# The roots of a norm spread by four transposes instead of a product with ones, and thirteen transposes of the identity at the start of TensorE's program

## The reference

```
n    = rmsnorm(x, ln1_g)                 # x * rsqrt(mean(x*x) + eps) * g
proj = n @ w_in                          # 1024 x 1536: pool, RG-LRU, gate
y_pool = pool_mixer(proj[:, :512])
y_lru  = rg_lru(conv(proj[:, 512:1024])) * gelu(proj[:, 1024:])
h    = x + concat(rmsnorm(y_pool), rmsnorm(y_lru)) @ w_out
h    = h + (silu(n2 @ w_gate) * (n2 @ w_up)) @ w_down      # n2 = rmsnorm(h)
out  = rmsnorm(h, lnf_g)
```

## Time and profile before

| what | value |
|---|---|
| runs of the kernel | 892.46, 892.58, 893.38 us (median 892.58) |
| profiled execution | 893.27 us |
| its span, first to last instruction | 891.4 us |
| PE busy | 880.2 us |
| DVE, ACT, POOL busy | 619.0, 394.1, 266.7 us |

### The profile page before, as it was taken

The page is one execution under the profiler, slowest core; times in us unless marked ns, Lnnn a source line. Parts: engine busy times, 40 slices in busy tenths (PEclk is TensorE's granted clock), DMA queues, the critical chain, the costliest instruction groups (busy, mean ns, idle before and its releaser), DMA issues.

```text
span 891.4 us, 11039 instructions
## 1 busy us (share of the span) xinstructions
PE 880.2 (99%) x3968; PEld 724.3 (81%) x3968; DVE 619.0 (69%) x866; ACT 394.1 (44%) x650; POOL 266.7 (30%) x208
## 2 busy tenths in 40 slices
PE   7999999999999999999999999999999999999997
PEld 6877788888888888888888888888888888888886
DVE  4778996655997956656565564655738975787667
ACT  6689733524555333233233232233334444454456
POOL 0000032723334555545555545555540000000000
PEclk9999999999999999999999999999999999999999
DMA  9033011133002423224232232423339933333334
GB/s 316 16 95 95 24 48 48 47 118 95 1 1 60 142 82 120 94 83 161 65 130 83 95 130 86 140 71 106 112 100 384 393 98 94 95 97 102 98 83 189
DMA packets 94318, 98.01 MB, mean 110 GB/s; under 512 B 5764, under 2 KB 63672, under 8 KB 94264
## 3 DMA queue, kind: packets, MB, share of 16 engines
q1 hardware_dynamic: 83736, 78.16, 26.2%
q10 hardware_dynamic: 10528, 19.15, 7.2%
HBM read 70.81 MB, written 24.38 MB: 107 GB/s over the span
## 4 chain that ended last, share of the span: by engine, by line
PE 98%; DMA 0%; DVE 0%; ACT 0%; issue 0%; DVEq 0%; ACTq 0%
PE bank L2212 23%; PE bank L2210 23%; PE bank L2211 23%; PE bank L2089 5%; PE bank L2096 5%; PE bank L2093 5%; PE bank L2018 3%; PE bank L2020 3%; PE bank L2019 3%; PE bank L2119 1%; PE bank L2061 1%; PE bank L2031 1%; DMA h<-in_x 0%; PE bank L2040 0%; PE bank L2102 0%
## 5 line engine op out<-in xcount | busy, mean ns | idle before, releaser
L751 POOL TENSOR_TENSOR r_lo<-gu_raw,r_hi 128x512 fp32r<-128x512 f32 x84 | 114.8, 1367 | 86.1 <-ACT r_hi L1051 86.1
L2210 PE MATMUL bank<-T_hi,r_lo 128*128 128x512 f32 x352 | 136.9, 389 | 0.0
L2211 PE MATMUL bank<-T_lo,r_hi 128*128 128x512 f32 x352 | 136.9, 389 | 0.0
L2212 PE MATMUL bank<-T_hi,r_hi 128*128 128x512 f32 x352 | 136.9, 389 | 0.0
L751 POOL TENSOR_TENSOR r_lo<-wsum_S,r_hi 128x512 fp32r<-128x512 f32 x66 | 98.1, 1487 | 114.8 <-ACT r_hi L1051 108.1
L2211 PE MATMUL bank<-d_lo,h_hi 128*128 128x512 f32 (+1 forms) x312 | 120.5, 386 | 0.0
L2212 PE MATMUL bank<-d_hi,h_hi 128*128 128x512 f32 (+1 forms) x312 | 120.5, 386 | 0.0
L2210 PE MATMUL bank<-d_hi,h_lo 128*128 128x512 f32 (+1 forms) x312 | 120.5, 386 | 0.0
L1051 ACT CAST r_hi<-gu_raw 128x512 fp32r<-128x512 f32 x84 | 52.0, 622 | 148.7 <-PE bank L2212 143.8
L2210 PE MATMUL bank<-nT_hi,r_lo 128*128 128x512 f32 x248 | 96.5, 389 | 0.0
L2211 PE MATMUL bank<-nT_lo,r_hi 128*128 128x512 f32 x248 | 96.5, 389 | 0.0
(11 more groups left out here) (250 smaller groups left out, 1610.2 us busy)
## 6 DMA issues: line engine op xcount, KB each, us to landing
h_raw<-hid_ops ACTq DMA_DIRECT2D x72, 256.0 KB, 2.6
gu_raw<-in_w_ffn_gate SPq DMA_DIRECT2D x22, 512.0 KB, 3.8
gu_raw<-in_w_ffn_up SPq DMA_DIRECT2D x22, 512.0 KB, 4.8
hid_ops<-hid SPq DMA_DIRECT2D x44, 256.0 KB, 2.3
dn<-in_w_ffn_down SPq DMA_DIRECT2D x44, 256.0 KB, 9.7
hid_ops<-hsum_S SPq DMA_DIRECT2D x33, 256.0 KB, 2.6
w_raw<-in_w_in SPq DMA_DIRECT2D x11, 512.0 KB, 4.4
h<-in_x SPq DMA_DIRECT2D x8, 512.0 KB, 6.5
```

The source lines that it names most:

```text
L751: pool.tensor_tensor(lo_of(n)[:], a_block(f, name), f32(hi_of(n)[:]), ALU.subtract)\
L2210: pe.matmul(bank, s_lo, m_hi, start=(opens and j == 0), stop=False, skip_group_check=True)
L2211: pe.matmul(bank, s_hi, m_lo, start=False, stop=False, skip_group_check=True)
L2212: ins = pe.matmul(bank, s_hi, m_hi, start=False, stop=(closes and j == n - 1), skip_group_check=True)
```

## The change

Two things, in one diff. (1) `diag` becomes `wide`: DVE multiplies ones instead of the identity by the root, so that each block has the root of a token in all columns of its partition, and TensorE transposes the four blocks into the four quarters of the bank. (2) TensorE no longer waits for the gains first: when `ident` is there it transposes `ident` seven times into bank 3, turns the gains, and transposes `ident` six more times. Bank 3 is not read before a later product opens it afresh.

```
-        diag = at("diag", 152.25, [P, HALF])
+        wide = at("wide", 152.25, [P, HALF])
...
             for t in range(4):
-                dve.tensor_scalar(diag[:, cols(t)], ident[:], rstd[:, t:t + 1], None, ALU.mult).then_inc(diag_ok, 1)
+                dve.tensor_scalar(wide[:, cols(t)], ones_sq[:], rstd[:, t:t + 1], None, ALU.mult).then_inc(wide_ok, 1)
...
+            def spin(times):
+                for _ in range(times):
+                    pe.transpose(psum[3][:, 0:P], ident[:], ident[:])
+
             pe.wait_ge(consts, 1)
+            spin(7)
             pe.wait_ge(g_rows_in, 16)
             pe.transpose(psum[2][:, 0:KT], g_rows[:], ident[0:KT, 0:KT]).then_inc(gT_ok, 1)
+            spin(6)
             for t in range(4):
                 first_transposes(t)
             project(0, 0)
...
             def broadcast_roots():
-                pe.wait_ge(diag_ok, 4)
-                pe.matmul(pg[0][:], ones_sq[:], diag[:], start=True, stop=True).then_inc(bcast_ok, 1)
+                pe.wait_ge(wide_ok, 4)
+                for t in range(4):
+                    ins = pe.transpose(pg[0][:, cols(t)], wide[:, cols(t)], ident[:])
+                ins.then_inc(bcast_ok, 1)
```

More of the change, by code:

```diff
@@ L288, in hymba_pool_rglru_block @@
         abs_ok, decay_ok = sem("abs_ok"), sem("decay_ok")
-        diag_ok = sem("diag_ok")
+        wide_ok = sem("wide_ok")
         var_ok = sem("var_ok")
```

## The result

The changed kernel takes 894.4 us (median of 22 runs, 892.28 to 896.55), the kernel before 893.05 us in the same comparison (22 runs, 892.42 to 893.7). The ratio is 1.0015, with a 95% interval of 1.0009 to 1.0021: slower, by a little, where 891.9 us and a range up to 893.0 had been predicted. The profiled execution of after took 893.95 us, with a span of 892.1 us, against 893.27 and 891.4 us before: this pair of traces differs by 0.7 us, the medians by 1.35, so the traces show where time goes and not the whole of the difference of the medians.

A forecast was written before the change was run, and what follows sets the result against it. PE, busy 880.2 of 891.4 us, was taken as the bound, with the start held by the low clock and loads of x. 893.27 - 0.96 (start) - 0.42 (roots) = 891.89, predicted 891.9 us, range 891.2 to 893.0.

The forecast's parts named there:

- 9.1 computed: Start: tile 3 of x lands at 9.10 us and becomes what bounds PE's transposes.
- part 1: Start: the thirteen identity transposes bring TensorE's clock rise forward, gaining 0.96 us that lasts to the end.
- rival 3: After the start: gaps let the clock fall back, products take 0.46 instead of 0.23 us; 6 us low gives 894.9; chance 0.04.
- Start: 0.96: Start: ACT's first `nT_hi` begins at 9.30 in place of 10.26 us, 0.96 us earlier, passing through to the end.
- 7.5: Start: TensorE's clock rises near 7.5 us; any rise up to about 8.1 us gives the same result.
- 0.15: Start: ACT begins about 0.15 us behind the start of the last transpose it needs.
- the gain was to be 0.3: Start, against the median of before: of a 0.7 us gain, 0.4 is the roots and the rest the start.
- lucky executions: Start: where the clock rises early, the old kernel too is held by tile 3, not under 892.31 us.
- Roots: 0.42: Roots: four transposes in place of the product with ones (0.86 us) save PE 0.42 us.
- Rival 1: Start: identity transposes don't bring the clock's rise forward; 892.98 us in an execution like the profiled one; chance 0.10.
- Less spread between executions: Whole kernel: run times should vary less than before, whose executions differ by 0.9 us.

The follow-up runs named there:

- few long: The changed kernel with two long products of the identity in place of the thirteen transposes (18 fewer TensorE instructions): 892.6 us, ratio 0.9995.
- roots alone: The changed kernel without the thirteen transposes of the identity, only the roots changed: 892.49 us, ratio 0.9993.
- before + 26 small: The kernel before with thirteen 8x8 transposes (26 instructions) added ahead of the gains: 894.6 us, ratio 1.0013.
- roots with two sums first: The changed kernel without the identity transposes, with VectorE's sums of lines 1785 and 1791 moved earlier in its order: 892.95 us, ratio 0.9997.
- after, sum first: The changed kernel with VectorE's sum u of block 2 moved ahead of the fourth weight sum and second hidden product: 893.44 us, ratio 1.0008.
- few long, sum first: few long with VectorE's sum u of block 2 moved ahead of the fourth weight sum and second hidden product: 892.38 us, ratio 0.9997.
- after, two sums first: The changed kernel with VectorE's sums of lines 1785 and 1791 moved earlier in its order: 892.72 us, ratio 0.9996.

## Why the prediction was wrong

**What bounds the kernel.** The reading of the start was right: PE waited three times, and tile 3's landing (9.05 us in after, 9.1 computed) became the bound. The step that failed is the end of part 1: "So 0.96 passes through to PE's first product and, since PE has no wait behind it, to the end." Waits behind the start were put at nothing, and one of 1.5 us arose at 302 us, where 1.8 us were lost. That PE has no wait says that nothing is late; it doesn't say by how much. VectorE's `u` had only 0.5 us of room, and it hangs on a transfer and a queue of 12.6 us of work. Two rows, VectorE's line 1785 and the matmul behind it, would have shown the room. They would not have shown what used it up: not the head start (few long has more of it, 1.20 us, and no wait), but the landing, held by 1.1 us, and the 1.1 us of line 1756 behind it.

**The cause was costed at nothing**: that thirteen transposes are also twenty-six instructions. I weighed their time and their wait and no more. Three kernels show it: warming of the same length with 18 instructions fewer is 1.8 us faster than after, the 18 put back as tiny ones make it 1.6 slower, and 52 more, which put the fetch ahead of the load, make after 1.9 faster. The kernel before with the 26 alone is 1.5 us slower by the median. No rival had this in it; the one that ended slower (rival 3) was another mechanism.

**Start: 0.96.** Measured 0.80 in the trace. The rise came between 6 and 7 us rather than at 7.5, which changes nothing, as worked out. ACT started 0.37 us behind the start of tile 3's first transpose, not 0.15: that row was taken from a pipelined group of four, and here TensorE starts from idle. Against the median the gain was to be 0.3 and is none that shows: few long 892.6, roots alone 892.49, on the same chip. The traces say why. The one trace of before was a late case: its loads fell to 140 ns at 10.6 us. In the other three traces without early warming (roots alone, before + 26 small, roots with two sums first) they did so at 9.4, 9.5 and 8.6 us, and PE's first product followed the landing of tile 3 by 1.98 to 2.0 us, just as in the eight with it; in before it was 2.7. There the old start too is bound by tile 3, as the prediction's sum says for lucky executions, and the warming has nothing to win. And tile 3 itself lands anywhere from 9.0 to 10.4 us over the twelve traces, so that after hit the computed 9.1 was partly luck.

**Roots: 0.42.** 0.86 became 0.44 in the trace; roots alone is 0.6 us under before by the medians (its interval includes no change). The term was right.

**The clock.** Rival 1, and with it the sentence of the Trainium skill (TensorE: Matmul & The Clock Gate, Part 4) that transposes don't bring the higher level: contradicted, the loads fell to 140 ns between 6 and 7 us with nothing but transposes before it. Rival 3, the fall-back, had 0.04 and is real: 12 of 98 runs of the eight kernels with early warming had a mean granted clock of 0.996 or 0.997, none of the 86 runs of before in the three groups nor of the 33 of the three kernels without. It costs 1.8 us when it comes (after, sum first: 895.04 against 893.26, medians of the two heaps), and rival 3's price of half the time spent low fits: 3.4 us low, 1.7. In after it is 2 runs of 22 (895.53 and 896.55), so it widens the spread and doesn't make the median. What decides it stays open. Two traces have the fall (after, sum first, at 11.9 us, and few long, sum first, at 12.4), each 0.4 to 0.6 us behind the start of the first product. They had idled 0.9 us for tile 3 and 0.85 us for the first `nT_lo`, but so had after, two sums first, without a fall. What sets the two apart is that their clock rose earliest of the twelve (loads of 140 ns from 5.1 and 5.6 us; the next is 5.8). The prediction's evidence against rival 3, an idle stretch of 1.2 us without effect, came before the rise and couldn't bear on it.

**Spread.** "Less spread between executions" was wrong: after spans 4.3 us, before 1.3. The clock's fall gives the two slowest runs. Whether each execution meets the collision is the other likely part, and no trace shows it for single runs of after: one of its runs took 892.28, and one of the 21 runs of before in the third group 894.76, both with a mean clock of 0.999.

## What to carry to other kernels

A list of waits shows what is late and not what is nearly late: compare the end of each thing that the busiest engine needs with the time when it comes, and ask what a transfer that lands 1 us late would do there. Count instructions as well as time; adding or dropping some on TensorE moved the later fetches of its instructions here (287.2 us in after, 280.2 with 52 more), and one may come down beside a transfer that somebody waits for. If such a change moves a time far from where it was made, pad the stream with a few tiny instructions before blaming the edit.

## What the runs showed that I had not expected

- A fetch of 16 KB of instructions at the wrong moment goes with one of the sixteen parts of a load coming late: 1.2 us in after (289.56 against 288.38), and moving it away or back changes the kernel's time by 1.5 to 1.9 us. The Trainium skill's sentence that the fetch is hidden (Runtime: NRT & Kernel Launch, Instruction fetch mechanics) holds for TensorE itself, which never waits for it here, and not for the load beside it.
- A late VectorE can cost twice: 1.1 us more because its operation met GpSimd's (1.77 in place of 0.68). That operation took 1.77 us in all five traces with the late landing, and 0.68 in the five others that keep VectorE's old order.
- One kernel can have two times with no difference in its mean clock: before with 26 small instructions, near 892.8 or near 894.8 us.
- TensorE's clock, once up at 5.1 us, can fall again at 11.9 us. No run of before shows a mean clock as low.
